# A transformer block pair in fp32: copies of the attention stacks made by DMA, low weight halves written piece by piece, and the stick-breaking branch started three units ahead on three score banks

## The chip, the core and the metric

The kernel runs on one core of a Trainium2 chip. The time is the device time of one execution in microseconds (us); less is better. The engines are TensorE (PE, with its weight loads as PEld), VectorE (DVE), ScalarE (ACT), GpSimd (POOL) and SyncE (SP), which here only issues DMAs. They run their own instruction streams and wait for each other by semaphores.

## The reference

Two transformer blocks on 512 tokens (plus 16 meta tokens in the first) and 1024 features, in fp32. The change touches the mixer of the second block:

```python
h = rms_norm_2(x, mix_norm)
fq, fk, fv, f_logit, sq, sk, sv, g_fox, g_sb = split_columns_2(h @ w_in)
# forgetting attention, 8 heads of 64: fq and fk are normed per head
F = cumsum(log_sigmoid(f_logit + forget_bias))
logits = q @ k.T * scale + F[query] - F[key]          # causal
y_fox = softmax(logits) @ v
# stick-breaking attention, 8 heads of 64, strictly causal
log_beta, log_1m = log_sigmoid(z), where(mask, log_sigmoid(-z), 0)   # z = q @ k.T * scale
after = cumsum(log_1m, reverse=True) - log_1m
y_sb = where(mask, exp(log_beta + after), 0) @ v
merged = sigmoid(g_fox) * (y_fox @ w_branch_fox) + sigmoid(g_sb) * (y_sb @ w_branch_sb)
```

## The kernel before

All products of fp32 matrices are made of three matmuls in the fp32r type (L546 to L548): high half of the weights by high half of the activations, high by low, low by high. Weights come in 174 numbered chunks of 1024 x 256. For each chunk c, SP loads `raw[c % 2]` in two DMAs of 512 KB, once POOL has finished the low half of chunk c - 2 (`w_lo`). ACT writes the high half `whi` (L1006, in the attention stages L1306 in three parts of 3, 3 and 2 eighths), POOL the low half `wlo` = raw - whi (`low`, L455, four instructions of 512 columns). PE then runs 48 matmuls of 512 columns per chunk, 24 for each half t = 0, 1 (k = 0 to 7), and DVE scales and stores each half of the result.

In the second block's mixer the attention is threaded into the chunks' matmuls. A chunk has six places for it, its **thirds** (after k = 2, 5 and 7 of each half). A head has four **units**, one for each block of 128 queries (q = 0 to 3), with 128 (q + 1) keys; unit n = 4 h + q. At step n of a branch every engine does its part of some units in a fixed order.

Forgetting stage: chunks C_SQ to C_SV + 1 (six), step n = 6 j + third. PE scores unit n + 2 (`fox_scores`, L867 to L869, banks 1 and 3), turns the probabilities of unit n (L897, banks 5 and 4) and runs a piece of the value product of the head before (`fox_piece`, L884 and L885, which for a head's first piece waits until all four units are copied). DVE finds the least logit of unit n + 2, ACT takes the exponential, DVE divides; ACT copies the turned unit n (`fpTh`, L1177), DVE writes its low half (`fpTl`, L1874). At n % 4 = 2 the operands of head (n + 6) / 4 are stacked. ACT's `stack_high` writes the high halves `q1`, `k1` (L1284, L1285), for this branch two more tiles from `q` and `sel` (L1287, L1288), and `k1` once more into the other 64 partitions (L1290). POOL's `stack_low` writes the low halves (L496, L497) in the other places. After the step ACT runs `high_part` in thirds 0, 1 and 2; POOL runs `low` in third 2, behind `stack_low`.

Stick-breaking stage: chunks C_GF to C_GS + 3 (eight). `SB_STEPS` puts one step in each of the first 18 thirds and later two in three thirds. PE's step n (`attention`, L947 to L949, L904, L910) scores unit n + 2 in bank 1 or 3 once DVE has read unit n (`lg_read`), waits for the copy of unit n - 1, runs a value piece of the head before, waits for the probabilities of unit n and turns them in bank 5. DVE caps unit n + 2 (`capped`, L1930) and then, for unit n + 1, takes the maximum, a scan from the right and a difference (L1936 to L1938). ACT copies the turned unit n (L1177), takes Exp and Ln of unit n + 2 (`softplus`, L1365, L1367) and Exp of unit n + 1 (L1372), then `stack_high` without L1287 and L1288. Both first heads of this branch are stacked in the last chunk of the forgetting stage: by ACT in third 0, by POOL behind the last `low`. PE's first two scores stand between the two stages.

The banks of the chunks' results are 0 and 2 in both stages. SP issues all weight loads in the order of the chunks.

Of the kernel before, what the change touches and what calls it, by code (L numbers as in the profile page):

```python
# [26 lines left out]
P = 128  # L27
D = 1024
DK = D // P
T = 512  # L30
# [72 lines left out]
def build(nc, I, out):  # L103
    with ExitStack() as ctx:
# [45 lines left out]
        def at(name, off, shape, dt=F32):  # L150
# [91 lines left out]
        w_lo = sem("w_lo")  # L242
        tile_done = sem("tile_done")
# [25 lines left out]
            "y_split", "st_hi", "st_lo", "o_half", "y_sum")} for k in ("dsa", "fox", "sb")}  # L269
# [36 lines left out]

        def near(h):

            return slice(HEAD_DIM * (h % 2), HEAD_DIM * (h % 2) + HEAD_DIM)

        def far(h):

            return slice(HEAD_DIM * (1 - h % 2), HEAD_DIM * (1 - h % 2) + HEAD_DIM)

# [12 lines left out]
        def _(sp):  # L327
# [108 lines left out]
        def _(pool):  # L436
# [54 lines left out]
            def stack_low(A, h, q, k, q1, k1, k2, chunks):  # L491

                z, r = h % 2, near(h)
                pool.wait_ge(w_lo, chunks)
                pool.wait_ge(A["st_hi"], 3 * h + 2)
# [3 lines left out]

            F = att["fox"]  # L500
            stack_low(F, 0, qF, kF, qt1, kt1, kt2, C_SQ)
            low(C_SQ)
            stack_low(F, 1, qF, kF, qt1, kt1, kt2, C_SQ + 1)
# [22 lines left out]
            stack_low(B, 0, qS, kS, sq1, sk1, sk2, C_GF + 1)  # L526
            stack_low(B, 1, qS, kS, sq1, sk1, sk2, C_GF + 1)
            fox_pair(3)
            for j in range(8):
                for third in range(6):  # L530
                    for n in SB_STEPS[6 * j + third]:
                        if stacked_at(n) is not None:
                            stack_low(B, stacked_at(n), qS, kS, sq1, sk1, sk2, C_GF + j + (1 if third < 3 else 2))
                    if third == 2 and j < 7:
                        low(C_GF + j + 1)
# [7 lines left out]
        def _(pe):  # L543
# [316 lines left out]
            def fox_scores(n):  # L860
# [3 lines left out]
                if q == 0:  # L864
                    pe.wait_ge(F["st_hi"], 3 * h + 3)
# [36 lines left out]
            def turn(n, q):  # L902
                for j in range(q + 1):
                    mm = pe.transpose(ps[:, 5, P * j:P * j + P], pu[:, n % UNITS, P * j:P * j + P], ident[:])  # L904
                return mm

            def value_piece(v):
                def piece(h, j):
                    o, r = ps[row(h):row(h) + HEAD_DIM, 7, :], row(h)
                    return pe.matmul(o[:, P * j:T], v[:, j, HEAD_DIM * h:HEAD_DIM * h + HEAD_DIM],  # L910
                                     fpT[h % 2][:, j, P * j:T], start=j == 0, stop=j == QB - 1)
                return piece

            def pair_split(A):
                def wait(h):
# [9 lines left out]
            for j in range(6):  # L925
                c = C_SQ + j

                def run(t, k):
                    if k in THIRDS:
                        fox_step(6 * j + 3 * t + THIRDS.index(k))  # L930
# [6 lines left out]

            B = att["sb"]

            def sb_scores(n):  # L940
                h, q = divmod(n, QB)
                w, z = P * (q + 1), h % 2
                b = 2 * (n % 2) + 1
                if q == 0:
# [1081 lines left out]
```

## Time and profile before

| | us |
|---|---|
| median of 3 runs | 2089.76 |
| lowest, highest | 2088.69, 2090.17 |
| the profiled execution, its own time | 2091.32 |
| its span, first to last instruction | 2089.5 |
| PE busy | 2047.4 (98%) |
| DVE, ACT, POOL busy | 884.4, 754.2, 999.9 |

The profile is that of one execution. An engine's idle time before an instruction is put down to what released it last. In groups the mean is that of one instruction. Matmuls are pipelined: a row shows one from its start to its modelled end, and the next may start earlier. The granted clock of TensorE is a share of its full speed.

### The profile page before, as it was taken

To read this page: it belongs to the slowest core of one execution; us is meant where nothing else is said; L and a number is where in the kernel's file an instruction comes from. 1 tells how busy PE (TensorE), PEld (TensorE's weight loads), DVE (VectorE), ACT (ScalarE), POOL (GpSimd) and SP (SyncE) were. 2 spreads that over 40 slices of the span, in tenths; PEclk is the share of its full clock that TensorE was granted. 3 is DMA by queue.
4 is the path that set the end of the run, shared out by engine and by line. 5 is a ranking of instruction groups with operands and counts; after the bars stand their busy time and mean duration, and the time that the engine had idled before them with its cause. 6 is when DMAs were issued, how large, how long until landed. Compare 5 with 4: busy or idle time off the path is not lost.

```text
span 2089.5 us, 26593 instructions
## 1 busy us (share of the span) xinstructions
PE 2047.4 (98%) x9561; PEld 1672.6 (80%) x9561; DVE 884.4 (42%) x1394; ACT 754.2 (36%) x1038; POOL 999.9 (48%) x753
## 2 busy tenths in 40 slices
PE   8999999999999999999999999998899999999999
PEld 7798887678888888888888887887577888888887
DVE  6778635534333322243333124465653533332114
ACT  6412224433322223332222234666654332222232
POOL 5345442134555544455555455544444555554543
PEclk9999999999999999999999999999999999999999
DMA  4232331023333323333332332112113333332232
GB/s 156 63 106 81 101 101 61 30 72 101 101 91 89 100 96 97 90 101 100 100 96 86 104 96 79 54 51 61 41 61 101 90 94 98 100 100 96 91 106 81
DMA packets 250057, 184.01 MB, mean 88 GB/s; under 512 B 7040, under 2 KB 247168, under 8 KB 249984
## 3 DMA queue, kind: packets, MB, share of 16 engines
q1 hardware_dynamic: 249296, 182.74, 29.0%
q8 instruction: 44, 0.72, 0.1%
q10 hardware_dynamic: 688, 0.31, 0.1%
q14 instruction: 29, 0.24, 0.0%
HBM read 180.93 MB, written 2.10 MB: 88 GB/s over the span
## 4 chain that ended last, share of the span: by engine, by line
PE 89%; DVE 4%; POOL 2%; ACT 2%; issue 1%; DMA 0%; SPq 0%; DVEq 0%; ACTq 0%; POOLq 0%
PE ps L546 27%; PE ps L548 27%; PE ps L547 27%; POOL wlo L455 2%; DVE sc L1436 1%; PE ps L767 1%; PE ps L752 1%; PE ps L833 1%; PE ps L835 1%; PE ps L834 1%; PE ps L910 1%; DVE pu L1937 0%; DVE ssum L1564 0%; DMA raw<-in_w_in 0%; PE ps L766 0%
## 5 line engine op out<-in xcount | busy, mean ns | idle before, releaser
L455 POOL TENSOR_TENSOR wlo<-raw,whi 128x512 fp32r<-128x512 f32 (+1 forms) x692 | 939.1, 1388 | 971.4 <-ACT whi L1006 917.8
L546 PE MATMUL ps<-xh,whi 128*128 128x512 f32 (+2 forms) x1912 | 736.7, 385 | 13.9 <-DVE xl L1436 8.7
L548 PE MATMUL ps<-xh,wlo 128*128 128x512 f32 (+2 forms) x1912 | 723.3, 378 | 0.0
L547 PE MATMUL ps<-xl,whi 128*128 128x512 f32 (+2 forms) x1912 | 722.9, 378 | 0.0
L1006 ACT ACTIVATE whi<-raw 128x2048 fp32r<-128x2048 f32 (+1 forms) x159 | 297.6, 1871 | 797.2 <-PE ps L548 794.7
L546 PEld LDWEIGHTS ps<-xh,whi 128*128 128x128 f32 (+1 forms) x1912 | 359.6, 188 | 83.9 <-issue 11.9
L548 PEld LDWEIGHTS ps<-xh,wlo 128*128 128x128 f32 (+1 forms) x1912 | 358.7, 188 | 68.3
L547 PEld LDWEIGHTS ps<-xl,whi 128*128 128x128 f32 (+1 forms) x1912 | 359.5, 188 | 64.7 <-issue 2.5
L1490 DVE TENSOR_TENSOR tmp<-ps,rs 128x512 f32<-128x512 f32 x148 | 102.1, 692 | 325.9 <-PE ps L548 308.6
L546 PE MATMUL ps<-fh,whi 128*128 128x512 f32 x528 | 205.4, 389 | 0.0
L547 PE MATMUL ps<-fl,whi 128*128 128x512 f32 x528 | 205.4, 389 | 0.0
L548 PE MATMUL ps<-fh,wlo 128*128 128x512 f32 x528 | 205.4, 389 | 0.0
L1436 DVE SCALAR_TENSOR_TENSOR hT<-ps,hT 128x512 f32 x40 | 27.6, 691 | 271.0 <-PE ps L548 270.0
L1515 DVE TENSOR_TENSOR tmp<-tmp 128x512 f32<-128x512 f32 x66 | 90.2, 1367 | 114.3 <-ACT tmp L1048 114.2
L547 PEld LDWEIGHTS ps<-fl,whi 128*128 128x128 f32 x528 | 99.1, 188 | 20.7
L546 PEld LDWEIGHTS ps<-fh,whi 128*128 128x128 f32 x528 | 99.1, 188 | 20.5
L548 PEld LDWEIGHTS ps<-fh,wlo 128*128 128x128 f32 x528 | 99.1, 188 | 20.5
L1011 ACT ACTIVATE xh<-hT,vec (+1 forms) x48 | 34.5, 725 | 125.3 <-DVE hT L1436 125.3
L1050 ACT ACTIVATE fh<-tmp 128x512 f32 x66 | 41.8, 633 | 101.2 <-DVE tmp L1515 101.2
L1518 DVE TENSOR_TENSOR fl<-tmp,fh 128x512 f32 x66 | 51.0, 773 | 61.2 <-ACT fh L1050 61.2
L1436 DVE SCALAR_TENSOR_TENSOR xl<-hT,vec,xh (+1 forms) x48 | 46.7, 982 | 57.0 <-ACT xh L1011 57.0
L1048 ACT ACTIVATE tmp<-tmp 128x512 f32<-128x512 f32 x66 | 40.4, 612 | 2.9 <-DVE tmp L1490 2.9
(296 smaller groups left out, 2178.1 us busy)
## 6 DMA issues: line engine op xcount, KB each, us to landing
raw<-in_w_in SPq DMA_DIRECT2D x90, 512.0 KB, 4.6
raw<-in_w_gate_up SPq DMA_DIRECT2D x44, 512.0 KB, 4.7
raw<-in_ffn_w_gate SPq DMA_DIRECT2D x44, 512.0 KB, 3.9
raw<-in_ffn_w_up SPq DMA_DIRECT2D x44, 512.0 KB, 5.1
raw<-in_ffn_w_down SPq DMA_DIRECT2D x32, 512.0 KB, 4.3
raw<-in_w_down SPq DMA_DIRECT2D x16, 512.0 KB, 3.9
raw<-in_ffn_w_down SPq DMA_DIRECT2D x16, 384.0 KB, 3.5
raw<-in_w_b SPq DMA_DIRECT2D x8, 512.0 KB, 4.0
```

Source lines behind the costliest of these rows:

```text
L455: ins = pool.tensor_tensor(wlo[:, c % 2, cs], raw[:, c % 2, cs], whi[:, c % 2, cs].bitcast(F32), ALU.subtract)
L546: pe.matmul(o, w_of(whi), xhi, start=first, stop=False)
L547: pe.matmul(o, w_of(whi), xlo, start=False, stop=False)
L548: return pe.matmul(o, w_of(wlo), xhi, start=False, stop=last)
L1006: act.activation(whi[:, c % 2, 0:n], raw[:, c % 2, 0:n], ACT.Copy).then_inc(w_hi, 1)
L1011: act.activation(one(xh, nn)[:, lo:TM], one(hT, nn)[:, lo:TM], ACT.Copy, scale=col(vec, lin(gain + n, per, i))).then_inc(xh_done, 1)
L1048: act.activation(tmp[:, 1, :], tmp[:, 0, :], ACT.Silu).then_inc(silu_done, 1)
L1050: act.activation(one(fh, lin(n, per, i)), tmp[:, 3, :], ACT.Copy).then_inc(h_hi, 1)
L1436: return dve.scalar_tensor_tensor(o, a, s, b, op0, op1)
L1490: dve.tensor_tensor(o, ps[0:o.shape[0], bank(c, t), :], rsx[0:o.shape[0]], ALU.mult).then_inc(acc_free, 1)
L1515: dve.tensor_tensor(tmp[:, 3, :], tmp[:, 1, :], tmp[:, 2, :], ALU.mult).then_inc(h_done, 1)
L1518: dve.tensor_tensor(one(fl, nn), tmp[:, 3, :], one(fh, nn).bitcast(F32), ALU.subtract).then_inc(h_split, 1)
```

## The change

It does four things. (1) `stack_high` keeps only the writes of `q1` and `k1`. SP copies the rest from tile to tile by DMA (`doubled`): `k1` to the other 64 partitions for every head, and for the forgetting branch `q1` into `q2` and `sel` into `q2`. SP waits for `st_hi` of the head, at fixed places between its weight loads; PE waits for the new semaphores `st_dup0` and `st_dup1` before a head's first score. (2) In both stages POOL writes the low halves in three parts, each behind ACT's part (`low_of_part`, semaphores `hi_part` and `lo_part`), with two instructions for each. (3) The stick-breaking branch runs one unit further ahead: score n + 3 on banks 1, 3 and 4, two banks (5, 6) for turned units, ACT's and DVE's parts shifted by one unit; a step turns its unit before the value piece. (4) Its first three scores, with DVE's and ACT's work on them, stand in thirds 2 to 4 of the last forgetting chunk, and its first two heads are stacked in the chunk before that, in thirds 0 and 3.

The diff, cut to what the text speaks of; DVE's functions are shifted in the same way (`capped(n + 3)`, `sb_unit(n + 2)`):

```diff
             return 7 - h % 2
 
+        def sb_bank(n):
+            return (1, 3, 4)[n % 3]
+
+        def sb_turn_bank(n):
+            return 5 + n % 2
+
         def near(h):
 
...
+
+        def part_rows(part):
...
-            for c0, o, n in ((C_FV, S_FV, 2), (C_SQ, S_SQ, 2), (C_SK, S_SK, 2), (C_SV, S_SV, 2), (C_GF, S_GF, 4), (C_GS, S_GS, 4)):
-                for j in range(n):
-                    square(c0 + j, w2, o + CW * j)
+            def doubled(A, h, k1, q1=None, q2=None):
+
+                z = h % 2
+                there = A[f"st_dup{z}"]
+                sp.wait_ge(A["st_hi"], 2 * h + 2)
+                sp.dma_start(k1[z][far(h), :].bitcast(F32), k1[z][near(h), :].bitcast(F32)).then_inc(there, 16)
+                if q2 is not None:
+                    sp.dma_start(q2[z][near(h), :].bitcast(F32), q1[z][near(h), :].bitcast(F32)).then_inc(there, 16)
+                    sp.dma_start(q2[z][far(h), :].rearrange("p (q t) -> p q t", q=QB).bitcast(F32),
+                                 sel[far(h), h:h + 1, :].to_broadcast([HEAD_DIM, QB, P])).then_inc(there, 16)
...
+            F, B = att["fox"], att["sb"]
+            square(C_FV, w2, S_FV)
+            square(C_FV + 1, w2, S_FV + CW)
+            second(0)
+            sp.wait_ge(consts, 16)
+            doubled(F, 0, kt1, qt1, qt2)
+            second(1)
+            doubled(F, 1, kt1, qt1, qt2)
+            second(2)
+            for j in range(6):
+                for third in range(6):
+                    if stacked_at(6 * j + third) is not None:
+                        doubled(F, stacked_at(6 * j + third), kt1, qt1, qt2)
+                    if third == 3:
+                        second(j + 3)
+                    if j == 4 and third in (0, 3):
+                        doubled(B, third // 3, sk1)
+            for j in range(5):
+                for third in range(6):
+                    for n in SB_STEPS[6 * j + third]:
+                        if stacked_at(n) is not None:
+                            doubled(B, stacked_at(n), sk1)
...
+            def low_of_part(c, part):
+
+                k0, k1 = part_rows(part)
+                if part < 2:
+                    pool.wait_ge(hi_part, 2 * (c - C_SQ - 1) + part + 1)
+                else:
+                    pool.wait_ge(w_hi, c + 1)
+                half = CW * (k1 - k0) // 2
+                for z in range(2):
+                    cs = slice(CW * k0 + half * z, CW * k0 + half * z + half)
+                    ins = pool.tensor_tensor(wlo[:, c % 2, cs], raw[:, c % 2, cs], whi[:, c % 2, cs].bitcast(F32), ALU.subtract)
+                ins.then_inc(lo_part if part < 2 else w_lo, 1)
...
+            def lowered(c, third):
+
+                return (lo_part, 2 * (c - C_SQ - 1) + third) if 0 < third < 3 else (w_lo, c if third == 0 else c + 1)
...
             for j in range(6):
                 for third in range(6):
-                    n = 6 * j + third
+                    n, c = 6 * j + third, C_SQ + j + 1
...
-                        stack_low(F, stacked_at(n), qF, kF, qt1, kt1, kt2, C_SQ + j + (1 if third < 3 else 2))
-                    if third == 2:
-                        low(C_SQ + j + 1)
-
-            B = att["sb"]
-            stack_low(B, 0, qS, kS, sq1, sk1, sk2, C_GF + 1)
-            stack_low(B, 1, qS, kS, sq1, sk1, sk2, C_GF + 1)
+                        stack_low(F, stacked_at(n), qF, kF, qt1, kt1, kt2, *lowered(c, third))
+                    if third < 3:
+                        low_of_part(c, third)
+                    if j == 4 and third in (0, 3):
+                        stack_low(B, third // 3, qS, kS, sq1, sk1, sk2, *lowered(c, third + 1))
             fox_pair(3)
             for j in range(8):
...
-                    pe.wait_ge(F["st_hi"], 3 * h + 3)
+                    pe.wait_ge(F["st_hi"], 2 * h + 2)
+                    pe.wait_ge(F[f"st_dup{z}"], 48 * (h // 2) + 48)
...
+            B = att["sb"]
+
+            def sb_qk(n):
+                h, q = divmod(n, QB)
+                w, z, b = P * (q + 1), h % 2, sb_bank(n)
+                if n >= 3:
+                    pe.wait_ge(B["lg_read"], n - 2)
+                if q == 0:
+                    pe.wait_ge(B["st_hi"], 2 * h + 2)
+                    pe.wait_ge(B[f"st_dup{z}"], 16 * (h // 2) + 16)
+                    pe.wait_ge(B["st_lo"], 2 * h + 2)
+                pe.matmul(ps[:, b, 0:w], sq1[z][:, P * q:P * q + P], sk1[z][:, 0:w], start=True, stop=False, skip_group_check=True)
+                pe.matmul(ps[:, b, 0:w], sq1[z][:, P * q:P * q + P], sk2[z][:, 0:w], start=False, stop=False, skip_group_check=True)
+                pe.matmul(ps[:, b, P * q:w], identr[:], strictr[:], start=False, stop=True,
+                          skip_group_check=True).then_inc(B["lg_ready"], 1)
+
+            def sb_piece(h, j):
+
+                r = near(h)
+                if j == 0:
+                    pe.wait_ge(B["pt_copy_a"], QB * (h + 1))
                     if h % 2 == 0 and h:
-                        pe.wait_ge(A["y_split"], h // 2)
-                return wait
+                        pe.wait_ge(B["y_split"], h // 2)
+                pe.matmul(ps[r, 7, P * j:T], vS[:, j, HEAD_DIM * h:HEAD_DIM * h + HEAD_DIM], fpT[h % 2][:, j, P * j:T],
+                          start=j == 0, stop=j == QB - 1).then_inc(B["pv_ready"], 1)
+
+            def sb_step(n):
+                h, q = divmod(n, QB)
+                if n + 3 < QB * HEADS:
+                    sb_qk(n + 3)
+                if n < QB * HEADS:
+                    if n == 1:
+                        pe.wait_ge(F["y_sum"], HEADS)
+                    if n >= 2:
```

## Rows read from the trace of the kernel before

**Rows 1.** The page: busy engines, and the chain's shares by engine.

```profile
PE 2047.4 (98%) x9561; PEld 1672.6 (80%) x9561; DVE 884.4 (42%) x1394; ACT 754.2 (36%) x1038; POOL 999.9 (48%) x753
...
PE 89%; DVE 4%; POOL 2%; ACT 2%; issue 1%; DMA 0%; SPq 0%; DVEq 0%; ACTq 0%; POOLq 0%
```

**Rows 2.** Windows: length, busy us of PE, PEld, DVE, ACT, POOL; clock; DMA share, GB/s.

```profile
1318.00:1429.50 111.50, 100.72 (x622) 89.12 (x621) 64.44 (x154) 71.46 (x164) 53.16 (x42) 1.00 0.18 54
1429.50:1578.00 148.50, 138.05 (x607) 96.44 (x607) 87.71 (x146) 86.44 (x174) 62.04 (x48) 0.99 0.18 56
```

**Rows 3.** PE's waits, 1318 to 1560 us: us in total, times, longest.

```profile
PE ps L947 <- DVE pu L1938: 7.0, 9, 1.7
PE ps L546 <- POOL wlo L455: 4.7, 5, 1.2
PE ps L884 <- ACT fpTh L1177: 2.5, 2, 1.5
PE ps L884 <- DVE fpTl L1874: 2.4, 2, 1.2
PE ps L947 <- POOL sk L497: 2.0, 1, 2.0
PE ps L833 <- POOL wlo L455: 1.2, 1, 1.2
PE ps L884 <- issue: 0.6, 2, 0.3
PE ps L910 <- ACT fpT L1177: 0.5, 1, 0.5
PE ps L904 <- ACT pu L1372: 0.2, 1, 0.2
```

**Rows 4.** Timeline of PE: start, length, line, operands [idle before, and releaser].

```profile
1332.72 0.47 PE L884 MATMUL ps<-fpTh,vF 128*128 128x512 f32 x1 [1.21 <-DVE fpTl L1874]
...
1333.26 0.39 PE L546 MATMUL ps<-xh,whi 128*128 128x512 f32 x1
1333.49 0.39 PE L547 MATMUL ps<-xl,whi 128*128 128x512 f32 x1
...
1337.00 0.50 PE L546 MATMUL ps<-xh,whi 128*128 128x512 f32 x1 [1.12 <-POOL wlo L455]
...
1450.82 0.50 PE L947 MATMUL ps<-sk,sq 128*128 128x512 f32 x1 [0.38 <-DVE pu L1938]
```

**Rows 5.** The window at the seam of the two stages, columns as in rows 2.

```profile
1429.70:1433.10 3.40, 3.38 (x11) 3.01 (x12) 1.52 (x5) 1.05 (x4) 3.25 (x3) 0.52 0.66 229
```

**Rows 6.** Timeline of ACT: stacking and the copy behind it; stacking, second stage.

```profile
1328.29 0.62 ACT L1285 ACTIVATE kt<-kF 64x512 fp32r<-64x512 f32 x1
...
1330.08 0.63 ACT L1290 ACTIVATE kt<-kF 64x512 fp32r<-64x512 f32 x1
...
1331.27 0.58 ACT L1177 ACTIVATE fpTh<-ps 128x512 fp32r<-128x512 f32 x1
...
1444.97 0.61 ACT L1285 ACTIVATE sk<-kS 64x512 fp32r<-64x512 f32 x1
```

**Rows 7.** Timeline of DVE: the low half behind that copy.

```profile
1331.88 0.69 DVE L1874 TENSOR_TENSOR fpTl<-ps,fpTh 128x512 fp32r<-128x512 f32 x1 [2.95 <-ACT fpTh L1177]
```

**Rows 8.** Timeline of POOL: the last of a head's stacking, then a chunk's low half.

```profile
1330.44 1.28 POOL L497 TENSOR_TENSOR kt<-kF,kt 64x512 fp32r<-64x512 f32 x1
1331.79 5.15 POOL L455 TENSOR_TENSOR wlo<-raw,whi 128x512 fp32r<-128x512 f32 x4
```

**Rows 9.** DMA issues: how many, KB each, median us from issue to landing.

```profile
hT<-in_h SPq DMA_DIRECT2D x8, 264.0 KB, 6.9
...
out<-hT SPq DMA_DIRECT2D x8, 256.0 KB, 2.0
```

**Rows 10.** Timeline of DVE: the scan of 256 columns, twice.

```profile
1435.59 0.69 DVE L1937 TENSOR_TENSOR_SCAN pu<-pu 128x256 f32<-128x256 f32 x1
...
1448.75 1.55 DVE L1937 TENSOR_TENSOR_SCAN pu<-pu 128x256 f32<-128x256 f32 x1
```

More of the change, by code:

```diff
@@ L489, in _, with stack_low @@
             low(C_FV + 1)
-            def stack_low(A, h, q, k, q1, k1, k2, chunks):
+            def stack_low(A, h, q, k, q1, k1, k2, low_sem, level):
                 z, r = h % 2, near(h)
-                pool.wait_ge(w_lo, chunks)
-                pool.wait_ge(A["st_hi"], 3 * h + 2)
+                pool.wait_ge(low_sem, level)
+                pool.wait_ge(A["st_hi"], 2 * h + 2)
                 pool.tensor_tensor(q1[z][far(h), :], q[r, h // 2, :], q1[z][r, :].bitcast(F32), ALU.subtract).then_inc(A["st_lo"], 1)
@@ L530, in _ @@
                 for third in range(6):
+                    c = C_GF + j + 1
                     for n in SB_STEPS[6 * j + third]:
                         if stacked_at(n) is not None:
-                            stack_low(B, stacked_at(n), qS, kS, sq1, sk1, sk2, C_GF + j + (1 if third < 3 else 2))
-                    if third == 2 and j < 7:
-                        low(C_GF + j + 1)
+                            stack_low(B, stacked_at(n), qS, kS, sq1, sk1, sk2, *lowered(c, third))
+                    if third < 3 and j < 7:
+                        low_of_part(c, third)
             run(C_MX, C_D[2], 2)
@@ L900, in fox_step @@
                     fox_piece(h - 1, q)
[L902 to L912, printed above, removed]
@@ L929, in run @@
                     if k in THIRDS:
-                        fox_step(6 * j + 3 * t + THIRDS.index(k))
+                        third = 3 * t + THIRDS.index(k)
+                        fox_step(6 * j + third)
+                        if j == 5 and 2 <= third < 5:
+                            if third == 2:
+                                pe.wait_ge(st_zero, 2)
+                                pe.wait_ge(F["exp_done"], QB * HEADS)
+                            sb_qk(third - 2)
                 if c < C_SV:
@@ L1300, in high_part @@
             def high_part(c, part):
-                k0, k1 = (0, 3, 6, DK)[part:part + 2]
+                k0, k1 = part_rows(part)
                 if part == 0:
@@ L1305, in high_part @@
                     act.wait_ge(tile_done, 2 * (c - 1))
-                ins = act.activation(whi[:, c % 2, CW * k0:CW * k1], raw[:, c % 2, CW * k0:CW * k1], ACT.Copy)
-                if part == 2:
-                    ins.then_inc(w_hi, 1)
+                act.activation(whi[:, c % 2, CW * k0:CW * k1], raw[:, c % 2, CW * k0:CW * k1],
+                               ACT.Copy).then_inc(hi_part if part < 2 else w_hi, 1)
             def fox_unit(n):
@@ L1347, in _ @@
             B = att["sb"]
-            for j in range(6):
-                for third in range(6):
-                    fox_step(6 * j + third)
-                    if third < 3:
-                        high_part(C_SQ + j + 1, third)
-                    if j == 5 and third == 0:
-                        act.wait_ge(acc_free, 2 * C_SV)
-                        act.wait_ge(f_lo, 2)
-                        stack_high(B, 0, qS, kS, sq1, sk1)
-                        stack_high(B, 1, qS, kS, sq1, sk1)
-            fox_pair(3)
             def softplus(n):
```

130 lines of the change are left out of this document (66 added, 64 removed).

## The prediction

> **What bounds the kernel now.** I read the page first. TensorE (PE) is busy for 98% of the span and carries 89% of the chain that ended last [rows 1]. So nothing on another engine shortens the kernel unless PE waits for it, and the change leaves PE its matmuls one for one. What it can win is the time in which PE stands idle or runs slowly. Second, the two stretches that it touches: the forgetting stage (chunks C_SQ to C_SV + 1, 1318 to 1429.5 us) and the stick-breaking stage (C_GF to C_GS + 3, up to some 1578 us). PE is idle there for 10.8 and 10.4 us, while the other engines are busy for 42 to 64% [rows 2]. Third, who is waited for. The view of waits shows 24 waits of 21.1 us in all in these stages [rows 3]:
>
> - L947, a score of the stick-breaking branch, for DVE: 7.0 us in 9 waits;
> - L546 and L833, a chunk's first matmul, for `wlo` of POOL: 5.9 us in 6;
> - L884, the first value piece of a head of the forgetting branch, for the turned probabilities (ACT, DVE, "issue"): 5.5 us in 6;
> - L947 for POOL's stacked low halves: 2.0 us, once, at the seam of the stages;
> - L910 and L904: 0.7 us.
>
> The view understates each. A matmul of 512 columns is drawn 0.39 us long, though the next starts 0.23 us after it [rows 4]; a wait is counted from the drawn end, so 0.16 us of it is hidden. 24 × 0.16 = 3.8, and the waits cost 21.1 + 3.8 = 24.9 us.
>
> Last, the clock. From 1429.7 to 1433.1 us it was granted at 0.52 of full, the 1.2 GHz level [rows 5]. It fell inside the 2.0 us wait at the seam, in which PE did nothing. Half speed over some 3.3 us costs 1.6 us. In all, 26.5 us are there to be won, and no more.
>
> **The change part by part.** *Copies moved from ACT to DMA.* Of the five activations of `stack_high` for a forgetting head three go (L1287, L1288, L1290), of the three for a stick-breaking head one. L1285 starts at 1328.29, L1290 ends at 1330.71, and only then, behind one `whi` part, does the copy L1177 start at 1331.27 on which the value piece L884 hangs [rows 6]. Without L1287, L1288 and L1290 (0.6 us each) ACT is about 1.9 us sooner at L1177; the wait was 1.21 + 0.16 = 1.4 us [rows 4]. The same pattern stands at the other four heads, with the same or smaller waits. At the sixth, both stick-breaking heads' stacking stood just ahead of the copy (six activations of 0.6 us); it goes a chunk earlier. All 5.5 + 6 × 0.16 = 6.5 us go. What is late next is DVE's `fpTl`, which takes 0.7 us behind ACT's copy [rows 7]. The copy would end at 1331.85 - 1.9 = 1329.95 and `fpTl` at 1330.7; PE asked at 1332.72 - 1.21 = 1331.5. That is 0.8 us to spare, less where two thirds of a chunk are shorter (k = 6 and 7 alone), so I leave 0 to 1.5 us for all heads.
>
> *Low halves piece by piece.* POOL now starts `low` when the third `whi` part is written and runs 5.15 us; PE meets it at 1337.00 after 1.12 us [rows 8, 4]. Afterwards 3/8 and 3/8 are done a third and two thirds earlier, and behind the last part lie only 2/8 of 5.15, about 1.3 us: `wlo` is ready 3.8 us sooner against waits of at most 1.2 + 0.16. Two more instructions per chunk cost POOL little, and POOL is half idle. Where a head is stacked in third 2, `stack_low` (two of 1.3 us [rows 8]) stands ahead of the last part, as it did ahead of the whole. All 5.9 + 6 × 0.16 = 6.9 us go.
>
> *Three units ahead on three banks.* Now DVE must take in unit n + 1 and finish unit n between two steps of PE, with ACT's Exp and Ln in between. Afterwards unit n was finished a whole step before PE asks for its bank or probabilities. That needs throughput, not latency. DVE is busy 87.7 us over the 32 units, 2.7 us a unit with everything else it does there; ACT the same, less a copy per head [rows 2]. A third of a chunk is 8 matmuls × 0.23 = 1.8 us of PE; the stage less its stalls, 148.5 - 12 = 136.5 us, leaves 136.5 - 48 × 1.8 = 50 us, or 1.5 us for each step, so a third with a step takes PE 3.3 us. So both keep up: 7.0 + 0.7 + 11 × 0.16 = 9.5 us go. In the first chunk, where ACT still catches up with the seam, I leave 0 to 2 us.
>
> *Stacking and the first three scores moved into the forgetting stage.* PE finds the first stacks long done: 2.0 + 0.16 us go, and with them, I expect, the 1.6 us of the slow clock. The three scores are the same work in another place. Units 32 to 35 of the forgetting branch don't exist, so ACT and DVE have room for them in thirds 2 to 4. The wait on `F["exp_done"]` is long met there; `F["y_sum"]` moves to the second step, a third after the last piece.
>
> *What is added.* 8 × 3 + 8 × 1 = 32 DMAs of 128 KB: three for each forgetting head, one for each stick-breaking head, on SP's queue. No row shows a transfer from tile to tile. The nearest are the store of 256 KB in 2.0 us and, at the other end, the loads of 264 KB at the start, with others before them, in 6.9 us [rows 9]. I take 2.4 us, near the lower row, because the copies are smaller, start alone and touch tiles like the store. The tightest users are the stick-breaking heads from the third on. The first such head is written by ACT (`k1`) at 1444.97 to 1445.58; PE's step 5, at 1450.82, is where its score will be needed (it was step 6) [rows 6, 4]. That is 5.2 us, less the stalls that vanish, for 2.4 us of DMA beside 2.6 us of `stack_low`. Hidden, with 0 to 1 us for the first such head. Where a copy is queued behind a weight load (the head stacked at step 10), up to 1.6 us more.
>
> SP now waits for `st_hi` between weight loads. Its loads used to be held by `w_lo` alone. By the code the load of chunk j + 3 is issued in chunk j and first read (`high_part`) in chunk j + 2; a delay of a third or two doesn't reach that, so it costs nothing. The transposes come before the value piece now; each step still changes once from one kind of matmul to the other, so I take nothing, ±0.8 us.
>
> **The sum.** 6.5 + 6.9 + 9.5 + 2.2 + 1.6 = 26.7, without the rounding the 26.5 above. Of the allowances (0 to 1.5, 0 to 2, 0 to 2.6) I take 2.2 us, a third, since each margin worked out above is positive. The gain is 24.3 us of the profiled execution's 2091.3 us (span 2089.5); the median of the runs is 1.6 us below it, and the difference carries over: 2089.8 - 24.3 = 2065.5 us.
>
> **The rivals.** *DVE becomes the bound in the dense part.* The low halves now fall into three thirds of each chunk, and a scan L1937 of 256 columns took 1.55 us with POOL at work against 0.69 without [rows 10]. If every scan pays 0.86 us, a unit costs DVE up to 2.7 + 0.9 = 3.6 us against the 3.3 us of PE, in the 18 thirds at the start that all hold a step: 18 × 0.3 = 5.4 us stay, and the time is about 2071. Against it: many of the 2.7 us are already such collisions, and POOL does no more than before, in shorter instructions. The Trainium skill has a rule that speaks for this rival (SBUF — State Buffer, "Who interferes with whom"): a VectorE instruction with two SBUF inputs and a GpSimd instruction that reads SBUF lock each other out for a whole instruction. The rows on the scans agree with it. By it shorter pieces make each block shorter, so it lowers this rival's price rather than raising it.
>
> *The copies land late: slower than before.* Each stick-breaking head from the third on has about 5.2 us for its copy. At d us the six lose 6 × (d - 5.2): at 6.9 us that is 10 us (2076), and from d = 9.3 us the whole gain is gone; at 11 us it would be 2100. For it: SP issues a head's copies in order behind weight loads. Against it: the store of 256 KB takes 2.0 us [rows 9]. The Trainium skill (DMA: Bandwidth & Descriptors, "Anatomy of one DMA") puts the fixed part at 2.0 us and the rest at bytes / 436 GB/s; an estimate by it is 2.3 us for 128 KB, which is no part of the sum. No run here shows a copy between tiles yet.
>
> *The waits only move.* The recurrence PE, DVE, ACT, PE stays as long as it is, and PE meets it at the transposes (L904) instead of the score: then the 9.5 us stay and the rest goes, 2075. Against it: with three units ahead nothing that PE asks for was started less than two steps before.
>
> *The slow clock comes back at another place.* 1.6 us, 2067; inside the main range.
>
> **How the numbers follow.** Forecast as worked out, with or without the slow clock: 0.72. DVE bound: 0.12. Waits only moved: 0.06. Copies late but still faster: 0.03; slower than before: 0.04. Nothing measurable: 0.03. The range runs from all gone with the best order of transposes, 2089.8 - 26.5 - 0.8 = 2062.5, to past the DVE rival, 2074. A measurement of this kernel tells apart about 0.2% (4 us). Faster by more: 0.93; within: 0.03; slower: 0.04.
>
> **What would show it.** Right: PE's waits between 1318 and 1560 us fall from 21.1 us to under 3; no L546 or L833 for `wlo`; no L884; PEclk 1.00 at the seam; the copies land within 3 us; the span's end comes 24 us sooner and nothing before 1300 us moves. Wrong: a row of PE waiting for a copy into `kt` or `sk`; L904 or the new score line with several us for DVE; scans of 256 columns with a mean well above 1.0 us; any wait of ACT for `raw`.

## The result, and the profile of the changed kernel

The changed kernel takes 2062.12 us (median of 4 runs, 2061.71 to 2064.12); the kernel before took 2089.32 us beside it (4 runs). The ratio is 0.9871, with an interval of 0.9854 to 0.9889: 27.2 us less. I had forecast 2065.5 us, with a range from 2062.5 to 2074: the direction and the places were right, and the gain is 2.9 us larger than the 24.3 us of the forecast. The time lies 3.4 us below the forecast and 0.4 us beyond the range's fast end. About 0.5 us of the 3.4 is the kernel before, whose median the forecast took as 2089.8 and which had 2089.32 in these four runs; the gain itself lies at the edge of what the range allowed (26.5 + 0.8 = 27.3 us).

The page of after, busy engines and the shares of the chain (rows 1 are its counterpart):

```profile
PE 2038.7 (99%) x9561; PEld 1670.4 (81%) x9561; DVE 883.7 (43%) x1394; ACT 734.4 (36%) x1006; POOL 1009.8 (49%) x779
...
PE 95%; DVE 3%; issue 1%; ACT 1%; DMA 0%; SPq 0%; DVEq 0%; ACTq 0%
```

The same number of matmuls, 32 activations fewer on ACT (1038 to 1006), 26 instructions more on POOL. The windows of after, columns as in rows 2; the stages now end some 28 us sooner, so the second window ends at 1550:

```profile
1318.00:1416.00 98.00, 98.00 (x623) 88.54 (x622) 67.29 (x158) 61.45 (x148) 57.37 (x55) 1.00 0.32 92
1416.00:1550.00 134.00, 133.86 (x605) 96.12 (x604) 83.21 (x141) 79.75 (x163) 66.78 (x59) 1.00 0.22 66
```

PE is idle for 0.14 us of 232, where it was idle for 21.2 of 260 [rows 2], and the clock is 1.00 in both windows. The view of PE's waits from 1310 to 1570 us has no row: all nine of rows 3 are gone. From the first forgetting score to the first mixing matmul before took 264.33 us and after takes 236.76: 27.57 us, that is, the whole gain. The spans of the two profiled executions differ by more, 29.6 us: 2.05 us of it arise in the first 32 us of the kernel, at waits for the first loads, so that the first score comes at 1317.63 us in before and at 1315.58 in after. That belongs to the execution and not to the change: `turn_first_before`, below, which has the code of before up to there, reaches it at 1315.79.

The transfers of after from 1300 to 1560 us (name, how many, KB each, median us from issue to landing):

```profile
raw<-in_w_branch_sb SPq DMA_DIRECT2D x3, 512.0 KB, 4.5
kt<-kt SPq DMA_DIRECT2D x8, 128.0 KB, 2.2
qt<-qt SPq DMA_DIRECT2D x8, 128.0 KB, 2.3
qt<-sel SPq DMA_DIRECT2D x8, 128.0 KB, 2.4
sk<-sk SPq DMA_DIRECT2D x8, 128.0 KB, 2.2
```

A copy from tile to tile takes 2.2 to 2.4 us in the median; the longest, issued right behind weight loads, takes 5.0 us (issued at 1397.83, landed at 1402.79). I had taken 2.4. Seven of the 32 take 3.9 us or more. The Trainium skill (DMA: Bandwidth & Descriptors, "Anatomy of one DMA") has a sum for DMAs that GpSimd issues, by which an estimate for this size is 2.3 us; these copies are issued by SP, and their medians come out the same. The 5.0 us behind loads are not in that sum.

### The profile page after: what moved, and what is told of

Read it like the earlier page. It is cut to its first block, busy times and chain, and to the rows that moved or that the text cites. A ratio compares the mean times of both kernels' runs of the same rounds, so it can differ in the third digit from the quotient of the medians.

```text
span 2059.9 us, 26668 instructions
## 1 busy us (share of the span) xinstructions
PE 2038.7 (99%) x9561; PEld 1670.4 (81%) x9561; DVE 883.7 (43%) x1394; ACT 734.4 (36%) x1006; POOL 1009.8 (49%) x779
## 4 chain that ended last, share of the span: by engine, by line
PE 95%; DVE 3%; issue 1%; ACT 1%; DMA 0%; SPq 0%; DVEq 0%; ACTq 0%
PE ps L608 29%; PE ps L610 29%; PE ps L609 29%; DVE sc L1502 1%; PE ps L988 1%; PE ps L829 1%; PE ps L895 1%; PE ps L814 1%; PE ps L897 1%; PE ps L896 1%; PE ps L960 0%; DVE ssum L1630 0%; PE ps L828 0%; PE ps L822 0%; PE ps L1002 0%
## 5 line engine op out<-in xcount | busy, mean ns | idle before, releaser
L500 POOL TENSOR_TENSOR wlo<-raw,whi 128x512 fp32r<-128x512 f32 (+1 forms) x640 | 870.6, 1391 | 923.3 <-ACT whi L1079 916.4
L608 PE MATMUL ps<-xh,whi 128*128 128x512 f32 (+2 forms) x1912 | 735.5, 385 | 9.3 <-DVE xl L1502 7.3
L609 PE MATMUL ps<-xl,whi 128*128 128x512 f32 (+2 forms) x1912 | 721.8, 378 | 0.0
L608 PEld LDWEIGHTS ps<-xh,whi 128*128 128x128 f32 (+1 forms) x1912 | 357.9, 187 | 91.7 <-issue 23.9
L609 PEld LDWEIGHTS ps<-xl,whi 128*128 128x128 f32 (+1 forms) x1912 | 358.3, 187 | 64.6 <-issue 2.5
L608 PE MATMUL ps<-fh,whi 128*128 128x512 f32 x528 | 205.4, 389 | 0.0
L609 PE MATMUL ps<-fl,whi 128*128 128x512 f32 x528 | 205.4, 389 | 0.0
L1502 DVE SCALAR_TENSOR_TENSOR hT<-ps,hT 128x512 f32 x40 | 27.6, 691 | 271.0 <-PE ps L610 270.0
L609 PEld LDWEIGHTS ps<-fl,whi 128*128 128x128 f32 x528 | 99.1, 188 | 20.6
L608 PEld LDWEIGHTS ps<-fh,whi 128*128 128x128 f32 x528 | 99.1, 188 | 20.5
L555 POOL TENSOR_TENSOR wlo<-raw,whi 128x384 fp32r<-128x384 f32 (+1 forms) x78 | 77.1, 1016 | 42.8 <-ACT whi L1374 41.8
```

What stands on the lines that cost most here:

```text
L500: ins = pool.tensor_tensor(wlo[:, c % 2, cs], raw[:, c % 2, cs], whi[:, c % 2, cs].bitcast(F32), ALU.subtract)
L555: ins = pool.tensor_tensor(wlo[:, c % 2, cs], raw[:, c % 2, cs], whi[:, c % 2, cs].bitcast(F32), ALU.subtract)
L608: pe.matmul(o, w_of(whi), xhi, start=first, stop=False)
L609: pe.matmul(o, w_of(whi), xlo, start=False, stop=False)
L1502: return dve.scalar_tensor_tensor(o, a, s, b, op0, op1)
```

## Experiments

Each kernel below computes the whole result. "Stage" is the stretch from the first forgetting score to the first mixing matmul: 264.33 us in before, 236.76 in after.

**The changed kernel again.**

> The changed kernel once more, beside the three that each hold one of its parts, so that all stand against the same runs of the kernel before. 2062 us by its first runs; with the value piece ahead of the turning, the kernel of the earlier experiment took 2060.5. Theory (turning first costs PE about 1.5 us, because a value piece behind a turned block starts about 0.2 us after it instead of 0.03): 2062 us again. Rival (the difference was one of chips): 2060.5 us.

2061.74 us (2061.55 to 2062.33), ratio 0.9868 (0.9852 to 0.9885), stage 236.73, again without a wait of PE. The excess over my forecast is no scatter.

**One part undone.** *Copies back on ACT* (`act_copies`):

```diff
-                there = A[f"st_dup{z}"]
-                sp.dma_start(k1[z][far(h), :].bitcast(F32), k1[z][near(h), :].bitcast(F32)).then_inc(there, 16)
...
+                if q2 is not None:
+                    act.activation(q2[z][r, :], q[r, h // 2, :], ACT.Copy)
...
+                act.activation(k1[z][far(h), :], k[r, h // 2, :], ACT.Copy).then_inc(A["st_hi"], 1)
```

> The changed kernel with the copies of the stacks back on ScalarE (five activations for a forgetting head, three for a stick-breaking head), no copy by DMA; low halves in parts and three units ahead stay. Theory (a head's first value piece waits for ScalarE's copy behind its stacking): the waits of L884's kind come back at five heads, 3.9 us drawn and about 5 us of time; 2067 us. Rival (with three parts of low halves and the lead, ScalarE has enough room, the copies were not worth moving): under 1 us, 2062 to 2063 us. Second rival: ScalarE falls behind in the dense part of the stick-breaking stage as well, over 8 us, 2070 us and more.

2068.98 us (2068.79 to 2069.37), ratio 0.9904 (0.9888 to 0.9921), 6.9 us above after; stage 243.95. PE's waits:

```profile
PE ps L925 <- DVE fpTl L1922: 2.7, 2, 1.5
PE ps L925 <- issue: 1.5, 3, 0.7
PE ps L925 <- ACT fpTh L1227: 1.0, 1, 1.0
PE ps L965 <- ACT fpT L1227: 0.9, 1, 0.9
```

L925 is the first value piece of a head (L884 of before). Its wait comes back with the copies, 5.2 us drawn where before has 5.5. Beside it stands one of 0.9 us at a value piece of the stick-breaking branch (L965), where before has 0.5 (L910); no wait for `wlo` or at a score is there. I had expected 5 us in all. This part is worth about what its waits were.

*Low halves whole* (`low_whole`), for the forgetting stage (the other stage in the same way):

```diff
-                    if third < 3:
-                        low_of_part(c, third)
+                    if third == 2:
+                        low(c)
```

> The changed kernel with POOL writing each chunk's low half whole behind the third high part, as before; copies by DMA and three units ahead stay. Theory (the part alone decides when wlo is ready): PE waits at the start of the same chunks; at least the 6.9 us of the forecast, and since PE now comes to a chunk's end sooner by the stalls that are gone, up to twice that: 2069 to 2076 us. Rival (the waits for wlo were a consequence of ScalarE's late third part and of POOL's stacking, which the copies cured): under 2 us, 2062 to 2064 us.

2079.41 us (2079.06 to 2080.04), ratio 0.9953 (0.9936 to 0.997): 17.3 us above after, far more than the 6.9 us that this part's waits cost in before, and 3.4 us beyond what I expected. Stage 254.0. PE's waits, then two windows:

```profile
PE ps L608 <- POOL wlo L500: 12.1, 6, 4.3
PE ps L895 <- POOL wlo L500: 1.0, 1, 1.0
```

```profile
1337.00:1340.40 3.40, 3.40 (x13) 2.89 (x12) 0.29 (x1) 0.00 (x0) 0.00 (x0) 0.50 0.93 296
1446.20:1449.60 3.40, 3.40 (x11) 2.65 (x10) 0.00 (x0) 0.00 (x0) 0.00 (x0) 0.50 0.82 258
```

The waits for `wlo` have grown from 5.9 to 13.1 us, the longest from 1.2 to 4.3. For the first of them the trace shows why: POOL's low half starts 14.2 us and ends 19.3 us after the first forgetting score, as in before, but PE, which has not waited at the head's value piece, asks for it after 16.8 us instead of 18.3. For the later ones I haven't worked it out. Behind the two longest waits (2.5 and 4.3 us) the granted clock was 0.50, the 1.2 GHz level, for 3.4 us each, which is 3.4 us of time again.

*Two units ahead, stacking at the seam* (`two_ahead`): the `attention` of before with its two score banks in the place of `sb_step` and `sb_qk`, and the first two heads stacked in the last forgetting chunk.

```diff
-                if n + 3 < QB * HEADS:
-                    sb_qk(n + 3)
...
+            qk, step = attention(B, "lg_read", sb_scores, turn, value_piece(vS), pair_split(B))
...
-                if n + 3 < QB * HEADS:
-                    softplus(n + 3)
...
+                    softplus(n + 2)
```

> The changed kernel with the stick-breaking branch put back: two units ahead on two banks, its first scores between the stages, its first two heads stacked in the last forgetting chunk; copies by DMA and low halves in parts stay. Theory (the lead takes away 7.7 us drawn, 9.5 us in all, and the seam 2.2 us and 1.6 us of slow clock): 13 us, 2075 us, with the clock low for about 3.3 us at the seam. Rival (fewer activations and earlier low halves already shorten the loop and the seam): about 5 us, 2067 us, and no slow clock.

2073.32 us (2073.17 to 2073.52), ratio 0.9924 (0.9908 to 0.9941), 11.2 us above after; stage 248.32. PE's waits:

```profile
PE ps L1013 <- DVE pu L1997: 7.8, 9, 1.5
PE ps L609 <- DVE vS L1876: 0.9, 1, 0.9
PE ps L948 <- issue: 0.4, 1, 0.4
PE ps L968 <- ACT pu L1432: 0.2, 1, 0.2
```

The score (L1013, L947 of before) waits for DVE nine times, as in before [rows 3]; the 0.9 us of a chunk's matmul for DVE (L609) is a wait that before doesn't have. `two_ahead` also has the order of before, with the value piece ahead of the turning, which is 1.5 us faster than the new one (`order_back`, below), so the lead and the seam by themselves are worth more than the 11.2 us, some 12.7 by this estimate. The expectation had 13 us, 1.6 of them for a slow clock that didn't come. The wait at the seam isn't there, although the stacking is back in the last chunk: it was POOL's whole low half, ahead of the stacking in POOL's order, that made the seam late. In `copies_only`, below, which has both as before, the wait is there again, and in `lows_only`, which has the stacking as before and the low halves in parts, it isn't:

```profile
PE ps L1013 <- POOL sk L543: 2.0, 1, 2.0
```

So cutting the low halves is enough to remove it; I had put it down to the move of the stacking alone. The move is enough by itself too: `lead_only`, below, and `low_whole` have whole low halves and no such wait.

**One part alone in the kernel before** (the same edits, the other way round).

> The kernel before with the copies of the stacks as DMAs alone; low halves whole, two units ahead. Theory (each of the three parts uncovers the waits of the others, above all those for the low halves: undoing the parts one by one cost 6.9, 17.3 and 11.2 us, 35.4 in sum, where all together bring 27.2): the 6.5 us of the head waits go, but PE comes sooner to waits for wlo, which grow; 2084 to 2087 us. Rival (the parts add up as in the forecast): 6.5 us, 2083 us.

> The kernel before with the low halves in parts alone; copies on ScalarE, two units ahead. Theory (the waits uncover each other; this part helps the others most): at least the 6.9 us of the forecast and the seam's 2.2 and 1.6 us, because POOL reaches the first stick-breaking stacks sooner; 2079 us. Rival (it only moves PE to ScalarE's late copies): 3 us, 2086 us.

> The kernel before with the stick-breaking branch three units ahead alone (its scores and first stacks moved into the forgetting stage too); copies on ScalarE, low halves whole. Theory (the waits for wlo take over what the lead frees): 13 us by the forecast's terms, less waits for wlo in the second stage that grow from 2.4 us to 6 and more; 2079 to 2083 us. Rival (the terms add up): 2076 us.

- copies alone: 2083.65 us (2081.85 to 2084.21), ratio 0.997 (0.9959 to 0.9982), 5.8 us gained;
- low halves alone: 2084.28 us (2082.43 to 2085.63), ratio 0.9975 (0.9964 to 0.9987), 5.1 us;
- lead and seam alone: 2082.17 us (2081.38 to 2084.79), ratio 0.9964 (0.995 to 0.9978), 7.3 us.

The copies alone came out just below what I expected (2084 to 2087), near the rival by which they bring their full 6.5 us (2083); the lead came out inside its range (2079 to 2083). The low halves alone missed what I expected of them (2079) by 5 us. Their PE waits, and then those of the lead alone:

```profile
PE ps L989 <- DVE pu L1978: 8.8, 9, 2.3
PE ps L925 <- DVE fpTl L1915: 2.7, 2, 1.6
PE ps L925 <- ACT fpTh L1219: 2.5, 2, 1.5
PE ps L925 <- issue: 1.5, 3, 0.7
```

```profile
PE ps L587 <- POOL wlo L479: 10.6, 6, 3.6
PE ps L925 <- DVE fpTl L1922: 2.4, 2, 1.2
PE ps L874 <- POOL wlo L479: 1.2, 1, 1.2
PE ps L925 <- ACT fpTh L1227: 1.0, 1, 1.0
```

In the first the score waits for DVE have grown (8.8 us where rows 3 have 7.0), and so have those of the value piece (6.7 for 5.5). In the second the waits for `wlo` have doubled (11.8 for 5.9) and the granted clock was at the 1.2 GHz level twice, for 6.8 and 3.4 us. A part alone hands some of its gain to the waits next in line, the low halves and the lead more than the copies. The gains, in us, worked out from the medians:

| | copies | lows | lead and seam | sum |
|---|---|---|---|---|
| alone | 5.8 | 5.1 | 7.3 | 18.2 |
| what undoing it costs | 6.9 | 17.3 | 11.2 | 35.4 |

All three together give 27.2 and 27.7 in the two measurements, more than the sum of the singles and less than the sum of the undoings. The column of the lead holds the slower order of the transposes, worth 1.5 us: without it I estimate 8.8 and 12.7 us there. The shares by part in my forecast (6.5, 6.9, and 9.5 + 2.2 with 1.6 for the clock) were shares of what the waits cost in before. For the copies they tell both numbers fairly well, for the lead and the seam what leaving them out costs but not what they give alone, and for the low halves neither.

**The order of the transposes.** `order_back` is the changed kernel with the value piece ahead of the turning again, in the stick-breaking branch:

```diff
                     sb_qk(n + 3)
+                if h >= 1:
+                    sb_piece(h - 1, q)
...
                     mm.then_inc(B["pt_ready"], 1)
-                if h >= 1:
-                    sb_piece(h - 1, q)
```

> The changed kernel with one thing put back: in a step of the stick-breaking branch PE runs the value piece before it turns the unit's probabilities. The forecast allowed 0.8 us either way for this order, and the measured gain is about 1 us more than all idle time and slow clock that the forecast had counted. Theory (each wait costs PE more than its drawn idle time and the 0.16 us behind it: the first matmul after a wait is itself about 0.1 us slower to the next): the order is worth nothing, 2062.1 us, and the stretch from the first forgetting score to the first matmul of the mixing chunks stays 236.8 us. Rival (the order of turning and value piece gives the missing 1 us): 2063.1 us and 237.8 us.

2060.46 us (2059.86 to 2061.11), ratio 0.9863 (0.9847 to 0.9879), stage 235.29: 1.5 us shorter than after in the stage, where both theories expected no gain. It is the fastest of all kernels here by its median, though its slowest run and the fastest of `after_again` (2061.55) are only 0.4 us apart. One step in after, timeline of PE (start, length, line, operands): tail of the score, one transposed block, piece, the chunk's next two matmuls:

```profile
1484.34 0.22 PE L978 MATMUL ps<-strictr,identr 128*128 128x128 f32 x1
1484.40 0.28 PE L1002 MATMUL ps<-ident,pu 128*128 128x128 f32 x1
1484.61 1.07 PE L988 MATMUL ps<-fpT,vS 128*64 128x512 f32 x2
1485.61 0.50 PE L608 MATMUL ps<-xh,whi 128*128 128x512 f32 x1
1485.94 0.39 PE L609 MATMUL ps<-xl,whi 128*128 128x512 f32 x1
```

And in `order_back`:

```profile
1483.55 0.22 PE L978 MATMUL ps<-strictr,identr 128*128 128x128 f32 x1
1483.69 1.07 PE L988 MATMUL ps<-fpT,vS 128*64 128x512 f32 x2
1484.70 0.33 PE L1004 MATMUL ps<-ident,pu 128*128 128x128 f32 x1
1484.78 0.47 PE L608 MATMUL ps<-xh,whi 128*128 128x512 f32 x1
1485.10 0.39 PE L609 MATMUL ps<-xl,whi 128*128 128x512 f32 x1
```

The piece starts 0.21 us behind a transposed block; a matmul of the chunk starts 0.08 us behind one. The way from the score's tail to the chunk is 0.06 + 0.21 + 1.00 = 1.27 us in after and 0.14 + 1.01 + 0.08 = 1.23 in `order_back`. And L609 starts 0.335 us behind L608 in after and 0.313 in `order_back`. Both turning and piece stand in 28 steps. Over these the way to the chunk is shorter in `order_back` by 0.02 to 0.05 us a step, 1.0 us in all, and the distance between the first two matmuls of the chunk by another 0.6. Some 0.1 us of that is lost again, for `order_back` has one wait in the stage where after has 0.14 us of idle time:

```profile
PE ps L988 <- ACT fpT L1250: 0.3, 1, 0.3
```

The stage differs by 1.47. I had priced the order at nothing, ±0.8, because "each step still changes once from one kind of matmul to the other". The change does happen once, but what it costs depends on what follows it.

Two more kernels asked how far this reaches. `turn_first_before` is the kernel before with the turning ahead of the piece; `pieces_first` is `order_back` with the piece first in the forgetting branch too (there the turning stood first in both kernels).

> The kernel before with one thing of the change: in a stick-breaking step PE turns the unit before it runs the value piece. Theory (the order costs PE about 1.5 us over the stage wherever it has no waits to hide it in): the stage is some 1.5 us longer less what the waits absorb; 2089.5 to 2091 us. Rival (turned blocks a little sooner shorten the loop on which PE waits here): 2 us faster, 2087.5 us.

> The faster order of the earlier experiment (stick-breaking branch: value piece, then turning), with the same order in the forgetting branch too, whose value pieces are of the fp32r type. Theory (what costs is a value piece of the fp32 type behind a turned block; behind or ahead of it an fp32r piece changes nothing): 2060.5 us, the stretch from the first forgetting score to the first mixing matmul stays 235.3 us, and no wait comes back, since the piece asks only 0.3 us sooner for a low half that is ready 0.8 us ahead. Rival (turning last is better everywhere): 1 to 1.5 us less, 2059 us. Second rival (PE now asks for the low halves too soon): waits at head starts, 2062 us and more.

`turn_first_before`: 2092.61 us (2091.47 to 2094.34), ratio 1.0015 (1.0006 to 1.0024), stage 266.77: 2.4 us longer there and 2.9 in the median, more than the 1.5. PE's waits in the stages are 22.4 us instead of 21.1, which is about the rest: in a kernel that waits, the order also moves the waits. `pieces_first`: 2061.33 us (2061.01 to 2062.07), ratio 0.9866 (0.9851 to 0.9881), stage 236.23: 0.9 us longer than that of `order_back`, in the medians too (the two were not run side by side, and the intervals of their ratios overlap). I had expected no change. The 0.3 us of wait at L988 is in both, so it has no part in this; the steps of the forgetting stage with both turning and piece are longer with the piece first, by up to 0.06 us each and 0.8 us in all. The rule "piece first" holds for the stick-breaking branch and not for the forgetting one, whose pieces are pairs of matmuls.

**Copies made late.** The rival on the other side was that the copies land too late. To price it, the copy of a stick-breaking head is made three (`late3`) or five times (`late5`), each behind the landing of the one before, and the score waits for the last.

```diff
-                sp.dma_start(k1[z][far(h), :].bitcast(F32), k1[z][near(h), :].bitcast(F32)).then_inc(there, 16)
+                for again in range(1 if q2 is not None else 3):
+                    if again:
+                        sp.wait_ge(there, 16 * (3 * (h // 2) + again))
+                    sp.dma_start(k1[z][far(h), :].bitcast(F32), k1[z][near(h), :].bitcast(F32)).then_inc(there, 16)
```

> The changed kernel with each copy of a stick-breaking head made three times, one after the other, so that it lands about 4.6 us later (6.8 us after its issue instead of 2.2). The trace of the changed kernel shows 1.3, 4.3, 3.7, 3.0, 7.2 and 7.9 us between the landing and the first score of the third to the eighth head. Theory (PE pays only what goes beyond that): 3.3 + 0.3 + 0.9 + 1.6 = 6 us, 2068 us. Rival (the forecast's price, 5.2 us for every head: 6 x (6.8 - 5.2) = 10 us): 2072 us. Second rival (a stall gives the later heads time, so that only the first pays): 3 us, 2065 us.

> The same with five copies, about 9.2 us later (11.4 us after the issue). Theory: 7.9 + 4.9 + 5.5 + 6.2 + 2.0 + 1.3 = 28 us, 2090 us, about the kernel before; with the slow clock after the long waits up to 2095 us. Rival (the forecast's price): 6 x (11.4 - 5.2) = 37 us, 2099 us. Second rival (stalls give later heads time): about 15 us, 2077 us. PE's waits name the copy into sk.

`late3`, about 4.6 us later: 2069.94 us (2068.97 to 2070.68), ratio 0.9908 (0.9892 to 0.9923), stage 243.71. `late5`, about 9.2 us later: 2098.1 us (2096.69 to 2099.31), ratio 1.0043 (1.0028 to 1.0059), stage 271.55. PE's waits in the stages, `late3` and then `late5`, each with one row only:

```profile
PE ps L979 <- DMA sk<-sk: 4.5, 2, 3.2
```

```profile
PE ps L979 <- DMA sk<-sk: 23.7, 6, 7.5
```

In after, from a copy's landing to the score that reads it there were 1.31, 4.27, 3.74, 2.98, 7.22 and 7.86 us for heads 3 to 8. By these margins 4.6 us more cost 3.3 + 0.3 + 0.9 + 1.6 = 6.1, and 9.2 us more cost 27.8; measured were 4.5 and 23.7, somewhat less, since a head that waited gives the later ones more time. My rival counted 5.2 us from the issue of a copy to its score, for every head; in after these are 3.5 us at the third head, 6.4, 6.7 and 5.2 at the next three and 10 at the last two. The rest of the 34.8 us by which the stage of `late5` grew is nearly all clock: of the 30.7 us at the lower level PE worked in 21.3, which cost it half of that, 10.6 us. The totals came out 2 us (`late3`) and 3 us (`late5`) above what I had expected. The window at the end of its first long wait and behind it:

```profile
1438.40:1445.20 6.80, 6.01 (x15) 3.85 (x16) 2.80 (x4) 1.61 (x4) 0.00 (x0) 0.50 0.50 158
```

Such a spell goes with each of the four waits of 4.3 us or more; it begins while PE still waits. Against `after_again`, 8.2 us of the gain are lost at 4.6 us of lateness and all of it, with 8.4 us on top of the kernel before, at 9.2. My rival's price, 6 × (d - 5.2) with d = 2.2 + 4.6 and 2.2 + 9.2, gives 9.6 and 37.2 us against 8.2 and 36.4 measured above `after_again`. That is close by luck, for two faults of it cancel: its margins are too narrow for most heads, so that its waits are too long (9.6 and 37.2 us, where the margins of after give 6.1 and 27.8), and it has no slow clock.

## Why the forecast missed by 2.9 us

The mechanism stood; terms of the sum were mis-sized. Most of what I had named for "right" is in the profile: no wait of PE in the stages, no `wlo`, no value piece waiting, clock 1.00 at the seam. Two signs are not there as I gave them: 7 of the 32 copies took 3.9 to 5.0 us to land, where I had written "within 3 us", though PE waited for none, and ahead of 1300 us the two profiled executions differ by 2 us (above). Of the rivals, "the waits only move" and "copies late" have no row. "DVE becomes the bound" fell as well. The scans of the stick-breaking stage by form (x8 each: sum in us, mean ns), before and then after:

```profile
L1937 DVE TENSOR_TENSOR_SCAN pu<-pu 128x384 f32<-128x384 f32 x8 | 10.5, 1309 | 0.3
L1937 DVE TENSOR_TENSOR_SCAN pu<-pu 128x512 f32<-128x512 f32 x8 | 9.8, 1225 | 0.3
L1937 DVE TENSOR_TENSOR_SCAN pu<-pu 128x256 f32<-128x256 f32 x8 | 8.1, 1014 | 0.3
```

```profile
L1994 DVE TENSOR_TENSOR_SCAN pu<-pu 128x512 f32<-128x512 f32 x8 | 10.8, 1351 | 0.3
L1994 DVE TENSOR_TENSOR_SCAN pu<-pu 128x384 f32<-128x384 f32 x8 | 9.0, 1131 | 0.3
L1994 DVE TENSOR_TENSOR_SCAN pu<-pu 128x256 f32<-128x256 f32 x8 | 6.8, 851 | 0.3
```

Together 28.4 us before and 26.6 after: the scans got shorter in sum, not longer, though those of 512 columns alone got longer. That the shorter pieces of POOL did this isn't shown: `order_back` has the same pieces, and there these scans take 28.5 us. The longest hold-up of a scan is 1.12 us before (2.08 us for 384 columns, 0.96 undisturbed) and 0.73 in after (1.42 for 256 columns, 0.69 undisturbed). The Trainium skill (SBUF — State Buffer, "Who interferes with whom") says that a VectorE instruction with two SBUF inputs and a GpSimd instruction that reads SBUF lock each other out for a whole instruction; hold-ups shorter than one instruction of POOL for a low half (1.36 us before, 0.90 and 1.07 in after, in the mean) agree with it.

Three steps of the sum were mis-sized. The first is the one that failed: it set the range's fast end as well.

**The hidden part of a wait: 24.9 us should have been 27.7.** I added 0.16 us to each wait drawn, from the 512-column matmul that is drawn 0.39 long and followed after 0.23. That holds only where such a matmul is the last before the wait. Before the first row of rows 4 stands a transposed block (before, and then the same place in after, where nothing waits):

```profile
1331.23 0.28 PE L897 MATMUL ps<-ident,pu 128*128 128x128 f32 x1
...
1333.02 0.40 PE L885 MATMUL ps<-fpTl,vF 128*128 128x512 f32 x1
```

```profile
1329.18 0.28 PE L960 MATMUL ps<-ident,pu 128*128 128x128 f32 x1
1329.21 0.48 PE L947 MATMUL ps<-fpTh,vF 128*128 128x512 f32 x1
1329.52 0.40 PE L948 MATMUL ps<-fpTl,vF 128*128 128x512 f32 x1
```

The block is drawn 0.28 us, but the piece may follow after 0.03, so 0.25 us are hidden. The wait at 1332.72 cost 1.49 - 0.03 = 1.46 us, where 1.21 are drawn and I had counted 1.37. And the matmul that comes out of a wait can itself hold up the next one. A score in before, coming out of its wait at 1450.82 [rows 4], and one in after that didn't wait:

```profile
1450.04 0.40 PE L548 MATMUL ps<-xh,wlo 128*128 128x512 f32 x1
...
1451.15 0.39 PE L948 MATMUL ps<-sk,sq 128*128 128x512 f32 x1
```

```profile
1483.88 0.39 PE L976 MATMUL ps<-sk,sq 128*128 128x512 f32 x1
1484.11 0.39 PE L977 MATMUL ps<-sk,sq 128*128 128x512 f32 x1
```

0.33 us against 0.23: another 0.1 us, which stands in no wait. I compared each of the 26 waits of before's trace (the 24 of the view and two of 0.1 us or less) with the median of the same three matmuls in a row without a wait:

| waits of before | drawn | cost before the matmul | behind it | in all | forecast |
|---|---|---|---|---|---|
| value piece L884, 6 | 5.5 | 6.9 | 0.0 | 6.9 | 6.5 |
| chunk's first L546, L833, 6 | 5.9 | 7.1 | 0.3 | 7.5 | 6.9 |
| score L947, L904, L910, 13 | 7.9 | 9.9 | 1.1 | 11.0 | 9.5 |
| seam, 1 | 2.0 | 2.2 | 0.1 | 2.3 | 2.2 |
| in all | 21.2 | 26.1 | 1.6 | 27.7 | 24.9 |

With the slow clock (1.5 us beside what the seam's line already has) 29.2 us were there to be won, where the prediction says "26.5 us are there to be won, and no more". My range's fast end was built on that sentence, as if the size of the hidden part were known and not an estimate from one pair of rows.

**The order of the transposes: nothing, ±0.8, was a loss of 1.5 us.** `order_back` shows it. It goes the other way, and without it the miss would have been 4.4 us.

**The allowances: 2.2 us for heads, chunks and copies that come late.** None was needed. (A third of the 6.1 us allowed, as the prediction has it, would have been 2.0.) The idle time of PE in both windows is 0.14 us. But one margin was thin: 1.31 us from copy to score, where I had 5.2 us less 2.4. The allowance was for a real risk that didn't come about.

29.2 - 1.5 - 0.1 = 27.6 us, against 27.57 in the stage. The medians differ by 27.2 here and by 27.7 in the repeated run.

What stays open: why the chip needs 0.21 us between a transposed block and the stick-breaking piece and 0.03 between one and the forgetting piece. The two pieces differ in type (fp32, where the trace has two instructions for a piece, and fp32r), in columns of the array (128*64 and 128*128) and in what they read, and no run separated these. And a mixture of both orders, with the turning first only where the wait for `pt_copy_a` would bite, wasn't tried.

## What to carry to other kernels

Price a wait by the start of its matmul against the same succession of matmuls without a wait somewhere in the trace, not by the drawn gap; here that was 1.3 times the gap, and with the clock 1.4 times. When several engines take turns in making the bound engine wait, don't judge a part by trying it alone: here the parts alone gave 18 us and all together 27.5, and a part left out cost up to two and a half times its own waits. A switch between kinds of matmul has a price that depends on its neighbours, so try both orders.

## What the runs showed of the hardware

- A score that comes out of a semaphore wait holds up its successor by 0.1 us (0.33 instead of 0.23 us; ten cases in before, 0.105 to 0.114). So does a chunk's first matmul behind a value piece (0.11, twice), less behind a transposed block (0.03, three times); a value piece doesn't (0.00).
- Around PE's longest waits the granted clock went to the 1.2 GHz level: for 3.4 us with waits of 2.0 (before), 2.5 (`low_whole`, `copies_only`), 2.8 (`lead_only`), 3.2 (`late3`) and 4.3 us (`low_whole`), for 6.8 us with waits of 3.6 (`lead_only`) and 4.3 to 4.9 (`late5`), and for 10.2 us with one of 7.5 (`late5`). With waits of 2.0 (`turn_first_before`, `copies_only`) and 2.3 us (`lows_only`) it stayed at 1.00. I had counted the clock as a matter of the seam alone; the runs show it with most of the long waits, and it is part of why undoing one part cost more than its own waits.
- A copy of 128 KB from tile to tile takes 2.2 us and keeps that time with three and five of them one behind the other (`late3`, `late5`: median 2.2), but up to 5.0 us right behind weight loads of 512 KB on the same queue.
